# A two-block model on one core: smaller masked copies in HGRN2, its line of work at one step a round, and one stream of attention heads begun three rounds later

## The reference, cut to what matters

```python
mix = jnp.concatenate([y_m, y_a, y_h], axis=-1)   # mLSTM, differential attention, HGRN2
x = x + jnp.einsum('bte,ed->btd', mix, w_out[l])
```

```python
diff = Bc[..., :, None, :] - Bc[..., None, :, :]
decay = jnp.exp(jnp.where(causal, diff, NEG_BIG))
A = jnp.einsum('bhtk,bhsk,bhtsk->bhts', qb, kb, decay)
o = A @ vb + (qb * jnp.exp(Bc)) @ S
```

## Time and profile before

| | us |
|---|---|
| median of 3 runs | 3610.74 (3610.21 to 3612.33) |
| the profiled execution | 3609.81 |
| its span, first to last instruction | 3608.3 |
| PE busy | 3397.4 (94%) |
| DVE busy | 1260.0 (35%) |
| ACT busy | 1128.3 (31%) |
| POOL busy | 1211.9 (34%) |
| mean granted clock of PE | 0.957 |
| L2196, masked copies, 56 of 128x512 | 0.713 each |

### The profile page before, as it was taken

The page is one execution under the profiler, slowest core; times in us unless marked ns, Lnnn a source line. Parts: engine busy times, 40 slices in busy tenths (PEclk is TensorE's granted clock), DMA queues, the critical chain, the costliest instruction groups (busy, mean ns, idle before and its releaser), DMA issues.

```text
span 3608.3 us, 37132 instructions
## 1 busy us (share of the span) xinstructions
PE 3397.4 (94%) x15674; PEld 2720.6 (75%) x15674; DVE 1260.0 (35%) x2034; ACT 1128.3 (31%) x1552; POOL 1211.9 (34%) x292
## 2 busy tenths in 40 slices
PE   7997899999987999999998999999999989769999
PEld 5675688886755888888887788887888867658887
DVE  6337430315365422222124441224121253663122
ACT  3244431323243432322223332223222233433222
POOL 2220244443210344444443334443444332024442
PEclk9998899999987999999999999999999999879999
DMA  4110133332200232333323223333433323023332
GB/s 126 59 59 1 47 94 94 98 95 71 70 24 12 71 105 94 94 94 93 105 83 110 70 72 92 105 105 111 133 89 99 92 78 119 1 59 97 101 90 75
DMA packets 462492, 296.76 MB, mean 82 GB/s; under 512 B 14328, under 2 KB 454318, under 8 KB 462270
## 3 DMA queue, kind: packets, MB, share of 16 engines
q1 hardware_dynamic: 453808, 277.09, 26.4%
q10 hardware_dynamic: 8518, 17.30, 1.4%
HBM read 285.97 MB, written 8.39 MB: 82 GB/s over the span
## 4 chain that ended last, share of the span: by engine, by line
PE 86%; DVE 10%; ACT 3%; issue 1%; POOL 0%; DMA 0%; SPq 0%; DVEq 0%; ACTq 0%
PE bank L675 25%; PE bank L676 24%; PE bank L677 24%; PE bank L417 8%; PE bank L717 1%; PE bank L719 1%; PE bank L718 1%; DVE ta L1537 1%; DVE scr L2196 1%; DVE x L1135 1%; DVE ta L1133 1%; DVE qkv L2475 0%; DVE ta L2472 0%; ACT u L1988 0%; DVE tb L2473 0%
## 5 line engine op out<-in xcount | busy, mean ns | idle before, releaser
L606 POOL TENSOR_TENSOR wlo<-raw,whi 128x2048 fp32r<-128x2048 f32 (+3 forms) x277 | 1174.0, 4238 | 2305.6 <-ACT whi L581 2305.6
L675 PE MATMUL bank<-xh,whi 128*128 128x512 f32 x2304 | 917.3, 398 | 20.2 <-DVE xl L1159 15.3
L676 PE MATMUL bank<-xl,whi 128*128 128x512 f32 x2304 | 901.3, 391 | 0.0
L677 PE MATMUL bank<-xh,wlo 128*128 128x512 f32 x2304 | 900.9, 391 | 0.0
L581 ACT ACTIVATE whi<-raw 128x2048 fp32r<-128x2048 f32 (+3 forms) x279 | 491.4, 1761 | 565.7 <-PE bank L677 537.1
L675 PEld LDWEIGHTS bank<-xh,whi 128*128 128x128 f32 x2304 | 435.1, 189 | 137.0 <-issue 30.3
L677 PEld LDWEIGHTS bank<-xh,wlo 128*128 128x128 f32 x2304 | 434.9, 189 | 92.7
L676 PEld LDWEIGHTS bank<-xl,whi 128*128 128x128 f32 x2304 | 435.4, 189 | 87.5 <-issue 1.4
L675 PE MATMUL bank<-ah,whi 128*128 128x512 f32 x1216 | 474.1, 390 | 5.2 <-POOL wlo L606 5.2
L676 PE MATMUL bank<-al,whi 128*128 128x512 f32 x1216 | 473.7, 390 | 0.0
L677 PE MATMUL bank<-ah,wlo 128*128 128x512 f32 x1216 | 473.5, 389 | 0.0
(11 more groups left out here) (384 smaller groups left out, 3209.9 us busy)
## 6 DMA issues: line engine op xcount, KB each, us to landing
raw<-in_ffn_w_gate SPq DMA_DIRECT2D x85, 512.0 KB, 4.0
raw<-in_ffn_w_up SPq DMA_DIRECT2D x85, 512.0 KB, 5.3
raw<-in_w_up SPq DMA_DIRECT2D x64, 512.0 KB, 4.7
raw<-in_w_down SPq DMA_DIRECT2D x64, 512.0 KB, 5.0
raw<-in_w_in SPq DMA_DIRECT2D x56, 512.0 KB, 4.7
raw<-in_ffn_w_down SPq DMA_DIRECT2D x64, 384.0 KB, 4.1
raw<-in_ffn_w_down SPq DMA_DIRECT2D x64, 320.0 KB, 3.8
raw<-in_w_out SPq DMA_DIRECT2D x16, 512.0 KB, 4.2
```

Source lines behind the costliest of these rows:

```text
L606: g.e.tensor_tensor(self.wlo[slot][:, 0:n], self.raw[slot][:, 0:n], self.whi[slot][:, 0:n].bitcast(F32), ALU.subtract).then_inc(self.lo_ma ...
L675: pe.e.matmul(bank, hi[:, at:at + P], xh, start=k == ks[0], stop=False)
L676: pe.e.matmul(bank, hi[:, at:at + P], xl, start=False, stop=False)
L677: last = pe.e.matmul(bank, lo[:, at:at + P], xh, start=False, stop=k == ks[-1])
```

## The change

There are three edits. The masked copy of a level now takes only the odd blocks of columns of the mask, of the bank and of `at[i][e]`: 4 x (64 / half) blocks of `half` columns, 256 in place of 512. `often` is gone, and the HGRN2 and output line takes one step a round. `other_heads` yields three times before its first step, on every engine.

```diff
--- before.py
+++ after.py
@@ -284,13 +284,6 @@
         if i % n == n - 1:
             for line in others:
                 next(line, None)
-
-
-def often(steps):
-
-    for i, _ in enumerate(steps):
-        if i % 4 != 1:
-            yield
 
 
 def run(steps):
@@ -2190,10 +2183,12 @@
                     v.e.tensor_tensor(qs[i], qs[i], q[i], ALU.mult).then_inc(done.tick("qs", l, i), 1)
                     v.e.tensor_tensor(ks[i], ks[i], k[i], ALU.mult).then_inc(done.tick("ks", l, i), 1)
                 for e in range(2):
-                    mask = self.level[:, n:n + 1, :].to_broadcast([P, NB, P])
+                    half = LEVELS[n]
+                    mask = self.level[:, n, :].rearrange("p (m h b) -> p m h b", h=2, b=half)[:, :, 1, :].unsqueeze(1).to_broadcast([P, NB, HD // half, half])
+                    asking = lambda t: t.rearrange("p (c m h b) -> p c m h b", c=NB, h=2, b=half)[:, :, :, 1, :]
                     v.wait_ge(pe, pe["level", l, i, n, e])
                     v.wait_ge(done, done["level", l, i, n - 1, e] if n else done["same", l, i, e])
-                    v.e.copy_predicated(blocks(at[i][e]), mask, blocks(both[e][:])).then_inc(done.tick("level", l, i, n, e), 1)
+                    v.e.copy_predicated(asking(at[i][e]), mask, asking(both[e][:])).then_inc(done.tick("level", l, i, n, e), 1)
                 yield
             dec = self.tiny[:, 16 + 4 * i:20 + 4 * i]
             for _ in range(4):
@@ -2686,6 +2681,8 @@
                     yield
 
         def other_heads():
+            for _ in range(3):
+                yield
             yield from heads(0, (2 - mine, 3 - mine, 4))
             self.heads_left -= 1
 
@@ -2697,7 +2694,7 @@
                     next(line)
             while not self.heads_begun:
                 yield next(line)
-            yield from weave((other_heads(), 1), (often(line), 1))
+            yield from weave((other_heads(), 1), (line, 1))
         run(weave((first_line(), 1), (second_line(), 1)))
 
     def tensor(self):
```

## The result

The changed kernel takes 3555.4 us (median of 4 runs, 3552.57 to 3556.02) against 3611.15 us for the kernel before on the same chip: ratio 0.9844, 95% interval [0.9827, 0.9861]. It is 55.7 us faster, where 22.4 were forecast, and outside the range 3564 to 3608. The profiled execution took 3556.02 us with a span of 3554.5. The kernel without `often` is shorter, so its lines stand 7 lower up to the step of the copies (L2155 was L2162, L1916 was L1923, L1981 was L1988, L1989 was L1996, L1958 was L1965, L668 was L675, L410 was L417), and from the copy on 5 lower (L2191 was L2196, L2254 was L2259).

The account below looks back on a forecast made before the run. It took the HGRN2 stretch as bound by hand-overs between in-order engines, DVE densest. Per layer 1.5 (copies and rounds) + 6 (overlap) + 5 (phase) - 1.3 (tables) = 11.2 us, 22.4 in two: 3588 us, range 3564 to 3608.

Parts of the forecast that it names:

- The place: All gain lies in the HGRN2 stretches, 264 to 413 us in layer 0 and 1031 to 1184 in layer 1.
- the count of rounds: HGRN2 takes 51 rounds plus 23 with heads only; changed, 68 rounds, then 9 with heads only.
- the copies: Half-sized masked copies in the HGRN2 levels save 5.5 us a layer; lower end nothing.
- One step a round: HGRN2 spread over 68 rounds hides more of its steps under the heads: 6 us a layer, bounds 0 and 15.
- addition: Step cost in the stretch stays fixed: spreading alone brings nothing; copies and rounds added up give 1.5 us a layer.
- Three rounds behind: Attention streams in opposite phase split the reduce and Exp bundles: 5 us a layer, bounds 0 and 10.
- The sum itself: Per layer in the stretch, 1.5 + 6 + 5 - 1.3 = 11.2 us, 22.4 in two.
- Rival A: The three streams overlap as the 23 idle rounds promise: 21.6 us a layer, 3567 us; chance 0.20.
- Rival D: Each round in the stretch keeps its hand-over cost: slower, 3643 us, or 3625 with half of it; chance 0.10.
- Rival C: The masked copies don't get cheaper, 5.5 us less gain a layer: 3599 us; chance 0.07.
- Table loads: Two more ACT loads a layer, at the first pair of heads' Sqrt: 2.6 us, half counted, 1.3.
- Rival E: PE's clock stays at half for more of the stretch, costing 6 us a layer: 3600 us; chance 0.07.

Follow-up runs that it names:

- e4: Kernel before with the line at one step a round and stream 0 three rounds behind, full copies: 3565.9 us.
- after: The changed kernel with all three edits, against the kernel before: 3555.4 us, ratio 0.9844.
- e1: Kernel before with only the half-sized masked copies: 3607.1 us, ratio 0.9992.
- e2: Kernel before with only the HGRN2 line at one step a round: 3586.4 us, ratio 0.9935.
- e5: Changed kernel with both head streams in step again: 3574.9 us, ratio 0.9914 to the kernel before.
- e7: Changed kernel with stream 0 seven rounds behind in place of three: 3589.8 us.
- e3: Kernel before with only stream 0 three rounds behind: 3613.3 us, ratio 1.0008.
- S: The edit that puts stream 0 three rounds behind; alone on the kernel before 3613.3 us.
- O: The edit that takes the HGRN2 line at one step a round; alone on the kernel before 3586.4 us.
- C: The edit that halves the masked copies; alone on the kernel before 3607.1 us.
- e6: Changed kernel with four HGRN2 steps in three rounds again: 3605.5 us, ratio 0.9988 to the kernel before.
- e13: Changed kernel with each level's Exp and matmuls in one round with z and copies, then an empty round: 3582.6 us.
- e15: Changed kernel with each level's gap in one round with Exp and matmuls, then an empty round: 3596.6 us.
- e9: Changed kernel with two of every four line steps in one round and one round left empty, still 68 rounds: 3584.7 us.
- e8: Changed kernel with the mask's odd columns stored side by side, so the copy reads them contiguously: 3557.6 us.
- e12: Changed kernel with first-two-level copies writing (layer 0) or reading the bank (layer 1) side by side, output wrong: 3555.6 us.

## Why the prediction was wrong

**What held.** The place (between and behind the two stretches the kernels differ by about 1 us, once either way), the count of rounds (51 and 23, then 68 and 9), and the copies: 5.5 us a layer were taken and 5.2 measured (e4 to after). That last agreement is partly luck, and part of it may be the clock (below). Two levels of seven saved nothing, so in the stretch the copies hold DVE for 12.7 us where the forecast had 18.5 less 7.1, and in the old order they are worth 1.5 us a layer (e1).

```profile
L2191 DVE COPY_PREDICATED scr<-level,bank 128x256 f32<-128x256 uint8 x28 | 12.7, 518 | 1.3 <-PE bank L410 1.2
```

**One step a round.** The forecast put 6 us a layer on top of addition, which gave nothing; e2 measures 23.8 us, 11.9 a layer. In layer 0, counted from 260 us, a round cost 2.28 us, addition would make that 1.15 + 1.13 x 51/68 = 2.00, and e2 has 1.92: 5 us from overlap, as forecast. Another 3 us are the end. The last six rounds and the output steps in them took 10.4 us, and six more steps at 0.7 us follow, together 14.6 where the sum had 6.9 + 10.6. These are the 8.0 us by which HGRN2's token transposes in layer 1 start earlier (1007.9 for 1015.9). The other 14.1 of e2's 22.1 us of span fall in layer 1, and I had doubled layer 0. From the token transposes to the last L1965 layer 1 took 167.4 us before and 150.8 in e2, against 162.8 and 150.4 in layer 0; the granted clock from there to the end of the last L1965 in layer 1 was 0.75 and 0.80.

**Three rounds behind: the step that failed.** I took 5 us a layer for the phase, bounded it by 10, and set 4.8 against it, for the tables and three rounds: about nothing net. Measured beside one step a round are 10 us net (e2 to e4, e5 to after) and by the estimate from e7 13 gross a layer. In layer 0 the 68 rounds from 260 us to F took 130.5 us in e2 and 118.1 in e4, 12.4 less. I had priced the bundle by one stream's reduces in it alone, and of the waits only the heads' two. These are the waits in layer 0 from 260 us to the end of the last L1965, in us:

| waits | before | e3 (S) | e2 (O) | e4 (O S) |
|---|---|---|---|---|
| ACT for the reduces (L1988) | 19.7 | 5.1 | 13.4 | 7.9 |
| DVE for the scores (L1923) | 15.4 | 9.7 | 11.6 | 3.7 |
| PE for the masked copies | 15.0 | 11.2 | 7.7 | 3.9 |
| ACT for HGRN2's gap (L2259) | 27.3 | 19.9 | 22.1 | 13.1 |
| ACT for the heads' token transposes (L1978) | 17.3 | 15.2 | 14.3 | 5.4 |
| DVE for HGRN2's Exp (L2170) | 8.6 | 7.0 | 7.3 | 1.2 |
| ACT for the transposed weights (L1996) | 7.0 | 24.6 | 9.0 | 24.0 |
| DVE for the heads' Exp (L1929) | 4.8 | 16.8 | 1.4 | 10.5 |

From e2 to e4 ACT's waits for the gap and for the heads' token transposes fall by 9 us each and DVE's for HGRN2's Exp by 6, and I had counted none of them. Part of it is at the very start: in e2 stream 1's token transposes (L1860) stand behind matmuls of stream 0 and begin at 265.1 us, in e4 at 259.6. The longest of these waits, ACT's for HGRN2's gap, I hadn't cited:

```profile
ACT ta L2259 <- DVE ta L2162: 27.3, 11, 5.1
```

But no sum of waits gives the price. Two of them rise, and in e3 the same ones fall, the first even further than in e4, and the kernel is no faster:

```profile
ACT u L1996 <- PE bank L1880: 24.6, 10, 5.7
ACT ta L2259 <- DVE ta L2162: 19.9, 8, 3.6
...
ACT u L1988 <- DVE tiny L1923: 5.1, 5, 2.7
```

So the runs show that the phase was sized at less than half, and that it also frees the third stream; which of these waits makes the 10 us isn't shown.

**The sum itself.** I added the three parts as if each had its price. Beside `often` C is worth 3 to 8 us and S -3 to 2, beside one step a round 10.5 to 11.5 and 19.5 to 20.5 (e1 to e6). With doubled steps the path runs through HGRN2's own hand-overs, which neither a shorter copy nor another phase mends; e13 to e15 show which: gap to Exp (41 us) and Exp to z (27), not copy to gap (8.5). In e1 F came no earlier although DVE had some 6 us less to do. Rival A had the direction (everything overlaps better) and 3567, still 12 us short; its reason, idle DVE in the last 23 rounds, is only part of it, since e9 leaves no such rounds and is 29 us slower. Rival D, a round that keeps its price, is out: 1.65 us where it needed 1.88 or more. Rival C came true for two levels of seven.

**Table loads.** Two more a layer were foretold, three came: ten in place of seven. The two are at the first pair of heads, as said (Sqrt at 309.32 and 314.88, Exp between). The third is in HGRN2's norm, where now an Exp of the heads falls between the loads for the gate and for the Sqrt; I had only looked at the heads' own.

```profile
352.29 1.28 ACT L1981 ACT_TABLE_LOAD   x1
...
355.05 1.28 ACT L1327 ACT_TABLE_LOAD   x1
...
357.63 1.28 ACT L1981 ACT_TABLE_LOAD   x1
```

**The clock.** Rival E had it fall; it rose. In the stretch the granted clock went from 0.78 to 0.84, and PE was busy 3375.7 us in place of 3397.4 with the same 15674 matmuls; outside the two stretches its busy time is the same within 1 us. That was not in my sum, and no run separates what the clock gave from what the order gave. Two readings bound it. In layer 0 the 12.4 us of S came at a clock of 0.78 (e2) and 0.77 (e4) from 260 us to F, so they aren't the clock's. But e8, with the order and the copy times of the changed kernel, had 0.76 in its profiled execution where the changed kernel had 0.83, and reached F 4 us later (376.7 for 372.6). From e4 to the changed kernel F comes 5.5 us earlier while the clock goes from 0.77 to 0.83, so in layer 0 the gain of the copies may be the clock's in good part.

```profile
260.00:376.70 116.70, 96.37 (x614) 65.31 (x612) 84.33 (x222) 58.71 (x133) 0.00 (x0) 0.76 0.00 1
```

e15, the slowest of the three, had 0.68 from 260 to 340 us where the changed kernel had 0.83:

```profile
260.00:340.00 80.00, 64.16 (x392) 45.49 (x391) 50.72 (x134) 32.32 (x72) 0.00 (x0) 0.68 0.00 1
```

```profile
260.00:340.00 80.00, 67.69 (x500) 48.33 (x499) 67.38 (x184) 39.98 (x97) 0.00 (x0) 0.83 0.00 1
```

PE was busy for 64 and 68 us and did 392 matmuls in e15, 500 in the changed kernel. So some of e15's 41 us may be the clock's too; no run takes that apart from its waits.

**What stays open.** Why three rounds are better than two by 17 us and than four by 8 has no single wait that explains it; the place of each head step beside each of the three steps of a level repeats only every 21 rounds, and that wasn't taken apart. Nor is it shown which part of the 55.7 us is the clock's. No version that was run beats the changed kernel.

## What to carry to other kernels

This is one kernel; where several in-order engines share streams of dependent steps, it suggests an order of work. First see that between a step and the one that needs it there is a round of other work, on the idle engines too: a wait there holds whatever stands behind it in that queue. Then put equal streams out of phase, and try more than one distance: three rounds gave 19.5 us here, two 2.5. The phase counted only once the first was so, and the shorter copies counted for more, so the parts of such a change must be priced together, from the hand-over that is bare, and not added.

## What the runs showed of the hardware

A masked copy of 128x256 fp32 from PSUM takes 0.43 us when its destination in SBUF is written in runs of at least four elements, and 0.71 to 0.79 when the runs are of one or two (the changed kernel, e8, e12); the full 128x512 took 0.71. Reading PSUM and the uint8 mask at every other element costs nothing. The products of L2161, not masked, write the same runs at 0.41 us, so the pattern alone doesn't do it; what in the masked copy does isn't shown. The prediction weighed a rule on cachelines. The Trainium skill, Advanced Engine Details and Errata, Memory Cachelines, says that a pattern in PSUM that isn't contiguous slows matmuls significantly. For a DVE read of PSUM with one element of each pair the trace of e12 shows no loss: a pair of copies takes 0.77 us, as with whole runs.
